# Four phases of a two-layer decoder step re-ordered: where selection rounds, normalised tiles, compression products and turned keys stand

## The reference

```
def layer_norm(x, g, b):                       # after each sub-layer
    mu = mean(x); var = mean((x - mu)**2)
    return (x - mu) * rsqrt(var + LN_EPS) * g + b

def compress(k, pe, w1, b1, w2):               # mixer C, once for keys, once for values
    ch = k in chunks of 16 tokens              # b c j g e
    ha = einsum('bcjge,jef->bcgf', ch, w1[:16])
    hb = einsum('bcjge,jef->bcgf', ch, w1[16:])
    const = einsum('je,jef->f', pe, w1) + b1
    h = gelu(ha[:, :-1] + hb[:, 1:] + const)
    return einsum('bcgf,fe->bcge', h, w2)

kc = compress(k rows, pe[0], ...); vc = compress(v rows, pe[1], ...)
pc = masked_softmax(q . kc * SCALE)            # 16 heads, 8 to a kv head
o_cmp = pc . vc                                # compressed branch
blocks = top_k(block sums of pc + bonus, 16)   # picks for the selected branch
o = g0 * o_cmp + g1 * o_selected + g2 * o_window
```

## Time and profile before

| | us |
|---|---|
| median of three runs | 2809.2 (2801.62 to 2817.05) |
| profiled execution | 2816.06 |
| its span | 2814.3 |
| sample_b | 371.6 to 613.3 |
| ffn0 | 986 to 1479.7 |
| compressed branch and its turning | 1615.1 to 1715.8 |
| sample_c | 1879.4 to 2226.2 |
| ffn1 | 2320 to 2807.4 |

### The profile page before, as it was taken

One profiled execution on the slowest core, in us unless ns is written; L12 is line 12 of the kernel. 1 busy time (PEld: TensorE's weight loads), 2 busy tenths in 40 slices (PEclk: granted clock), 3 DMA queues, 4 the chain that ended last, 5 costly groups with the idle time before them and its releaser, 6 DMA issues. The chain is left out here.

```text
span 2814.3 us, 41116 instructions
## 1 busy us (share of the span) xinstructions
PE 2243.7 (80%) x15442; PEld 1833.4 (65%) x15442; DVE 1336.9 (48%) x2667; ACT 910.1 (32%) x1497; POOL 140.7 (5%) x405
## 2 busy tenths in 40 slices
PE   5895755547767789998977777967888778999896
PEld 1895323325535689997867775545666568999784
DVE  2222437874656435554452215853444544555444
ACT  0210222211236235453331104752333313454332
POOL 0001000000000111110010000000000011111001
PEclk9997767768889889999988857987999888999998
DMA  2455166513132065564204232124333206656321
GB/s 62 139 189 176 25 207 225 188 49 144 66 120 93 9 195 200 194 212 139 79 8 134 91 50 68 54 82 116 128 136 136 75 6 196 209 191 222 119 76 41
DMA packets 166928, 341.04 MB, mean 121 GB/s; under 512 B 37726, under 2 KB 104334, under 8 KB 162810
## 3 DMA queue, kind: packets, MB, share of 16 engines
q1 hardware_dynamic: 151584, 200.99, 23.0%
q10 hardware_dynamic: 11756, 83.75, 8.6%
q0 software_dynamic: 3456, 54.53, 5.0%
HBM read 312.33 MB, written 97.35 MB: 146 GB/s over the span
## 5 line engine op out<-in xcount | busy, mean ns | idle before, releaser
L216 PE MATMUL ffn_acc<-x_h,ffn_wh 128*128 128x288 f32 x1408 | 303.8, 297 | 6.0 <-DVE ffn_wl L208 6.0
L216 PE MATMUL ffn_acc<-x_l,ffn_wh 128*128 128x288 f32 x1408 | 302.9, 297 | 0.0
L216 PE MATMUL ffn_acc<-x_h,ffn_wl 128*128 128x288 f32 x1408 | 302.9, 297 | 0.0
L216 PEld LDWEIGHTS ffn_acc<-x_h,ffn_wh 128*128 128x128 f32 x1408 | 228.8, 190 | 6.2 <-issue 6.2
L216 PEld LDWEIGHTS ffn_acc<-x_l,ffn_wh 128*128 128x128 f32 x1408 | 228.7, 190 | 0.0
L216 PEld LDWEIGHTS ffn_acc<-x_h,ffn_wl 128*128 128x128 f32 x1408 | 228.5, 190 | 0.0
L1720 PE MATMUL ffn_acc<-ffn_wh,x_h 128*128 128x512 f32 x440 | 175.4, 399 | 22.1 <-DVE ffn_wl L208 22.1
L208 DVE TENSOR_TENSOR ffn_wl<-ffn_w,ffn_wh 128x2048 fp32r<-128x2048 f32 (+1 forms) x88 | 154.3, 1755 | 69.8 <-ACT ffn_wh L1748 69.8
L1721 PE MATMUL ffn_acc<-ffn_wl,x_h 128*128 128x512 f32 x440 | 173.2, 394 | 0.0
L1722 PE MATMUL ffn_acc<-ffn_wh,x_l 128*128 128x512 f32 x440 | 173.1, 393 | 0.0
L208 DVE TENSOR_TENSOR x_l<-ffn_hid,x_h 128x1152 fp32r<-128x1152 f32 x44 | 59.8, 1358 | 165.1 <-ACT x_h L1806 165.1
(11 more groups left out here) (409 smaller groups left out, 4744.7 us busy)
## 6 DMA issues: line engine op xcount, KB each, us to landing
out_s_b_kv<-state_b_kv ACTq DMA_DIRECT2D x80, 768.0 KB, 7.8
ffn_w<-ffn_up SPq DMA_DIRECT2D x44, 1024.0 KB, 10.5
ffn_w<-ffn_down SPq DMA_DIRECT2D x44, 512.0 KB, 3.7
sb_k<-state_b_kv SPq DMA_DIRECT2D x8, 2048.0 KB, 11.5
sb_v<-state_b_kv SPq DMA_DIRECT2D x8, 2048.0 KB
proj_ab_w<-w_in_ab SPq DMA_DIRECT2D x11, 1024.0 KB, 5.3
proj_c_w<-w_in_c SPq DMA_DIRECT2D x7, 1024.0 KB, 5.5
hT_ab<-proj_ab_stage ACTq DMA_DIRECT2D x22, 288.0 KB, 2.1
```

The lines of the kernel that those rows point to most:

```text
L216: done = pe.matmul(o, weights, x, start=start, stop=stop)
```

## The change

Four parts, in four phases.

1. *sample_b_phase*: `select` takes a first round and a number of rounds. Per request two rounds stand behind the shift, one behind the copies of `pT`, one behind the scaling; `mix_in` of a request follows at once instead of behind the next shift.
2. *ffn_phase*: the down-products of the last three groups (`LATE`) run with the tile as the outer loop. VectorE takes tile `t` in, then the factors of `t - 1`, then the gain of `t - 2`; ScalarE the root of `t` and the scaling of `t - 1`. The turns of ffn0 follow after all.
3. *prompt_compressed_phase*: `w1` and `pe` are loaded at the end of the projection's SyncE queue (`load_phi`). Key branch and value branch stand in the two halves of the partitions; 64 products of 65 columns, the 65th being `pe`, give hidden sums and constant at once. Scores take two heads a product (8 of 128 rows a tile), two tiles ahead; the values come out turned and ScalarE copies them to `mixT`, so `mix_c` and `turn_mix_phase` go.
4. *sample_c_phase*: a third bank `tps`; the hidden sums go into two of the three logit banks; the `x` turns are spread among the score products of the request before; the second half of the hidden products alternates with the key turns ahead of the probabilities; GpSimd copies the value part of `kv` (128x2048) to `v`, and the next gather into that buffer waits for this copy and the key turns, not for the values. ScalarE copies keys ahead of the gelu.

```diff
@@ sample_b_phase, VectorE
-                if b:
-                    mix_in(b - 1)
-                    select(dve, b, 0)
+                select(dve, b, 0, 2)
                 dve.wait_ge(turned_p, b + 1)
...
-                select(dve, b, 1)
+                select(dve, b, 2, 1)
...
                 dve.tensor_scalar(o[:, :], outp, rinv[:, b % 2:b % 2 + 1], None, ALU.mult).then_inc(scaled, 1)
-            mix_in(NB - 1)
+                select(dve, b, 3, 1)
+                mix_in(b)
@@ ffn_phase, TensorE
+            for n in range(NF - LATE):
                 pe.wait_ge(d_low, 2 * n + 2)
                 for j in range(2):
                     for t in range(NT):
+                        last = down(n, j, t)
...
             pe.wait_ge(tail_out, NF // 2)
+            for t in range(NT):
+                for n in range(NF - LATE, NF):
+                    if t == 0:
+                        pe.wait_ge(d_low, 2 * n + 2)
+                    for j in range(2):
+                        down(n, j, t)
@@ ffn_phase, VectorE
-            for t in range(NT):
-                take_in(1, t)
-                dve.wait_ge(summed, NT + t + 1)
-                norm.statistics(dve, t, 1)
-                norm.aggregate(dve, t, NT + t + 1)
-            for t in range(NT):
-                norm.factors(dve, t)
-            for t in range(NT):
-                norm.gain(dve, t)
+            for t in range(NT + 2):
+                if t < NT:
+                    take_in(1, t)
+                    dve.wait_ge(summed, NT + t + 1)
+                    norm.statistics(dve, t, 1)
+                    norm.aggregate(dve, t, NT + t + 1)
+                if 1 <= t <= NT:
+                    norm.factors(dve, t - 1)
+                if t >= 2:
+                    norm.gain(dve, t - 2)
@@ prompt_compressed_phase
+def load_phi(nc, sp, io, w1, x, loaded):
+        for a in range(2):
+            r = slice(a * HD, (a + 1) * HD)
+            sp.dma_start(w1[r, :, :], io["phi_w1"][a].rearrange("j e f -> e j f")).then_inc(loaded, 16)
+            sp.dma_start(x[r, 2 * SEQ:], io["phi_pe"][a].rearrange("j e -> e j")).then_inc(loaded, 16)
...
-                for j in range(32):
-                    last = pe.matmul(psc[0:HD, a:a + 1], w1e[:, a, j, :], peT[:, a, j:j + 1], start=(j == 0), stop=(j == 31))
...
+            for j in range(2 * STRIDE):
+                for a in range(2):
+                    r = slice(a * HD, (a + 1) * HD)
+                    last = pe.matmul(psh[r, 0:2 * CH + 1], w1[r, j, :], x[r, j:j + STRIDE * 2 * CH + 1:STRIDE], start=(j == 0), stop=(j == 2 * STRIDE - 1))
...
-                for h in range(N_HEADS):
-                    last = pe.matmul(lgp[i % 2][:, h * 32:(h + 1) * 32], q[:, h, i * P:(i + 1) * P], kcT[:, h // 8, :], start=True, stop=True)
+                for m in range(KC):
+                    last = pe.matmul(lgp[i % 2][:, m * 64:(m + 1) * 64], q[:, m, i * P:(i + 1) * P],
+                                     kc[:, m // 4, :, :].rearrange("r two c -> r (two c)"), start=True, stop=True)
...
+                    for half in range(2):
+                        r = slice(half * HD, (half + 1) * HD)
+                        last = pe.matmul(out[half][:, u * P:(u + 1) * P], v_blk[r, u // 2, :], pT[r, i % 2, u * P:(u + 1) * P], start=True, stop=True)
@@ sample_c_phase
-            e.wait_ge(tps_out[n % 2], n // 2 + 1)
+            e.wait_ge(tps_out[n % 3], n // 3 + 1)
...
+            for c in range(NB):
+                pool.wait_ge(kv_in[c % 2], 16 * (c // 2 + 1))
+                if c:
+                    pool.wait_ge(slc_out, c)
+                pool.tensor_copy(v[:, :, :], kv[:, c % 2, :].rearrange("p (j n) -> p j n", j=STRIDE)[:, :, 384:512]).then_inc(v_ready, 1)
+                if c + 2 < NB:
+                    pool.wait_ge(v_ready, c + 1)
+                    n = turn_no[("k", c, 3)]
+                    for m in range(n - 2, n + 1):
+                        pool.wait_ge(tps_turned[m % 3], m // 3 + 1)
+                    gather(c + 2)
...
+                    for f in range(4):
+                        hidden(c, 1, f)
+                        turn_k(c, f)
                 if b >= 0:
                     turn_p(b, 0)
```

More of the change, by code:

```diff
@@ L1119, in sample_b_phase, with select @@
         selection = SampleSelection(p, score)
[L1121 to L1125, removed]
+        def select(dve, b, first, rounds):
+            each = selection.ROUNDS // NB
+            for r in range(first, first + rounds):
+                selection.round(dve, b * each + r)
         block = p.body.enter_context(nc.Block())
@@ L1407, in low_part @@
                      self.keep.xh[:, 4 * half:4 * half + 4, lo:lo + w]).then_inc(self.low, 1)
[L1410 to L1430, removed]
 def output_phase(nc, name, w_out, g, b, keep):
@@ L1708, in turn_tail, with down @@
                 last.then_inc(tail_turned, 1)
-            for n in range(NF):
+            def down(n, j, t):
                 h, f2 = divmod(n, NF // 2)
+                f = 2 * f2 + j
+                if h and f == 0:
+                    pe.wait_ge(summed, t + 1)
+                tile = slice(t * P, (t + 1) * P)
+                wide, part = (wdh[:, n % 4, j, :], wdl[:, n % 4, j, :]), (hh[:, n % 3, j, tile], hl[:, n % 3, j, tile])
+                pe.matmul(down_acc[t][:, :], part[0], wide[0], start=(f == 0), stop=False)
+                pe.matmul(down_acc[t][:, :], part[0], wide[1], start=False, stop=False)
+                last = pe.matmul(down_acc[t][:, :], part[1], wide[0], start=False, stop=(f == NF - 1))
+                if f == NF - 1:
+                    last.then_inc(product, 1)
+                return last
+            for n in range(NF - LATE):
                 pe.wait_ge(d_low, 2 * n + 2)
                 for j in range(2):
-                    f = 2 * f2 + j
                     for t in range(NT):
[L1716 to L1725, removed]
+                        last = down(n, j, t)
+                if n % (NF // 2) < NF // 2 - 1:
                     last.then_inc(wd_used, 1)
@@ L1951, in prompt_compressed_phase @@
         tps = p.ps("tps", [P, 512])
-        outp = p.ps("outp", [P, 2 * 512])
-        names = ("loaded", "gated", "const_sum", "const", "hidden", "activated", "keyed", "values", "cleared", "placed",
-                 "scored", "soft", "exped", "weighed", "turned", "copied", "attended", "mixed")
-        (loaded, gated, const_sum, const, hidden, activated, keyed, values, cleared, placed,
-         scored, soft, exped, weighed, turned, copied, attended, mixed) = (p.sem(n) for n in names)
+        out = [p.ps(f"out{i}", [P, 512]) for i in range(2)]
@@ L2159, in sample_c_phase @@
             if b + 1 < NB:
-                turns += [("x", b + 1, i) for i in range(8)]
+                turns += [("x", b + 1, i) for i in range(8)] + [("k", b + 1, i) for i in range(4)]
             if b >= 0:
@@ L2395, in _ @@
                 if c < NB:
-                    for f in range(4):
-                        hidden(c, 1, f)
-                    for i in range(4):
-                        turn_k(c, i)
                     turn_kw(c)
@@ L2454, in _ @@
                 if c < NB:
+                    for i in range(4):
+                        turned(("k", c, i), kT[:, i * 512:(i + 1) * 512])
+                    act.copy(kT[:, PAST:LS], k_new[:, 0, c * NS:(c + 1) * NS]).then_inc(kT_new, 1)
                     for a in range(2):
```

318 lines of the change are left out of this document (167 added, 151 removed).

## The result

The changed kernel takes 2693.27 us (median of 4, 2687.19 to 2699.18) against 2812.03 of the kernel before (median of 4); the ratio is 0.958, 95% interval 0.955 to 0.962: 119 us less, where 107.5 were forecast (2704, range 2675 to 2750). Measured again beside other kernels (last experiment) the ratio was 0.957 (0.955 to 0.959). The profiled execution took 2687.2 us, its span 2685.4.

| phase | before | after | difference | forecast |
|---|---|---|---|---|
| sample_b | 241.7 | 208.5 | -33.2 | -29 |
| ffn0, first to last work | 493.6 | 488.0 | -5.6 | -4 |
| compressed branch, first load to the next phase's | 101.3 | 58.3 | -43.0 | -46 |
| sample_c | 346.8 | 314.8 | -32.0 | -21 |
| ffn1, first to last work | 487.2 | 478.6 | -8.6 | -7.5 |

What follows compares the result with a forecast made beforehand. Barrier-closed phases on one core, each priced by itself: VectorE bounds sample_b, TensorE sample_c, serial tails the rest. -29 - 11.5 - 46 - 21 = -107.5 gives 2708.6 from 2816.1, 2701.7 from 2809.2; forecast 2704, range 2675 to 2750.

Steps and rivals of the forecast that it cites:

- sample_b, -29: In sample_b, moving one selection round per request into VectorE's wait cuts the period from 26.60 to 22.5 us; -29 us.
- the hole: In sample_b, VectorE's 4.73 us idle time per request ahead of the shift, while TensorE does the logit products.
- Rival (e): In sample_b, rounds move but key loads or ScalarE's copies keep the period at 26; nothing gained, 2733; chance 0.05.
- Feed-forward tails, -11.5: Serial work behind each feed-forward phase's last product shortens: ffn1 -7.5 us, ffn0 about -4, together -11.5.
- TensorE's wait: In each feed-forward phase, TensorE waits about 1.05 us for the last hidden group's high and low parts before tile 0.
- Compressed branch, -46: Prompt's compressed branch loses one-column products, a wait and the turning phase; next phase loads at 1669.3, not 1716.4; -46 us.
- Rival (b): In the compressed branch, quarter products don't run beside one another: 7 us more in hidden products, 0.8 a tile; 2714; chance 0.12.
- sample_c, -21: In sample_c, a third bank and earlier key copies remove waits for ScalarE's copies: -3 us a period, seven periods, -21.
- the slow stretch: In sample_c, 6.9 us of each period at granted clock 0.51; a period of 36.2 us if it stays, 33.2 at full clock.
- Rival (a): In sample_c, the slow stretch stays, from thinly spaced products around the picks: -1.4 a period, 11 us less gain, 2715; chance 0.17.
- (c): In sample_c, GpSimd's value copy of 8.7 us holds up VectorE's pair sum ahead of the picks: 26 lost, 2730; chance 0.08.
- (d): In sample_c, GpSimd's copy at 25 ns a column makes a 57 us loop against 37.6: +140 us, 2865; chance 0.03.

Runs made afterwards that it cites:

- last experiment: The changed kernel itself, run again on the same chip beside two kernels with respread sample_b rounds: 2693.82 us, ratio to before 0.957.
- the experiment on their order: Changed kernel with all 32 key-quarter products ahead of all 32 value-quarter products, not alternating: products 14.24 us against 7.44, branch 65.7 instead of 58.3.
- the two orders put back: Changed kernel with sample_c's third score products again ahead of the importance and x turns again in pairs: 2713.7 us, phase 339.3 instead of 314.8.
- one order alone: Kernel before, only sample_c's third score products moved behind the window's values of the request before: 2817.9 us, phase 349.1.

## Why the forecast held, and where its terms were off

*sample_b, -29, measured -33.* The step held: one round fills the hole, and the wait ahead of the shift is gone. Mis-sized was the period, 22.5 for 21.84: the logit products were taken at the 4.5 us of the earlier trace rows, and the copies of the turned probabilities at 17 behind the scaling; the granted clock in the phase is 0.87 after and was 0.76, so the shift begins 5.28 us behind the scaling and not 5.75, and the copies stand at 16.4 and, in four of the seven periods, wait for nothing. Rival (e) falls, since the period moved with the rounds.

*Feed-forward tails, -11.5, measured -14.* TensorE's wait was 1.06 us, as forecast. The gains were taken at 2.01 us each; two of the three took 1.23 and 1.21, since GpSimd's part was over by then or within 0.1 us of it, and the tails are 1.6 and 1.1 us shorter than forecast.

*Compressed branch, -46, measured -43* (58.3 us from its first load to the next phase's, 54 forecast). The steps held up to the last tile: hidden products 7.44 for 7.0, first softmax 21.4 us behind the first load for 20.6, 8.9 us a tile for 9.1. Missed was a queue: the last tile's exponential stands on ScalarE behind the copy of the third tile's turned probabilities, and VectorE waits 2.36 us for it; turn, values and barrier took 6.97 us for 5.3, 1.7 more than taken. Rival (b), quarters that take turns, falls with the experiment on their order.

*sample_c, -21, measured -32 to -36.* This is the term that was mis-sized, by its step "if the slow stretch stays, it is 36.2; between -4.4 and -1.4 I take -3": a midpoint between two outcomes, of which one came about. The stretch did not stay at all; the period is 32.8, as laid out for full clock (33.2; a turn with its hidden products took the 1.68 us taken). Rival (a), that the stretch stays, did not come about, and its reading of the stretch does not hold: the products in it weren't thin, TensorE is busy 6.43 of the 6.90 us of the earlier trace rows. The idle time ahead of them is the better candidate, for with the two orders put back the gaps and the stretch come again together; but one period with 4.5 us of idle time ran at full clock (1968.25 to 2003.68 above), so it is argued and not shown. And one step was wrong that the total could not show: of the two things said to take away the waits, the third bank does nothing. Which part of the new order takes away the wait for the keys was not run by itself.

*GpSimd's copy.* 1.89 us, near the memset of the earlier trace rows, not the 4 taken nor the bounds above. So (c) and (d) did not come about; (c)'s mechanism is real and has a margin of 3 us, the time between the copy's end and the pair sum.

## What to carry to other kernels

In a phase that TensorE bounds, price the waits and the granted clock apart: compare a period with the slow stretch and one without it in the same kernel (37.98 and 35.43 us here). Look at the idle gaps ahead of a slow stretch before blaming the products in it, and check in the profile that a moved product really filled a gap: the one moved by itself here filled none, and its run could not decide what it was made for. When a bound goes, lay out the chain that is late next before moving more work off the old one: a round less on VectorE was worth 1.1 us a period until the turn was moved too. A copy on an idle engine is free only as long as it ends before the other engine's short instructions that it lengthens (0.63 us to 3.51 here).

## What the runs showed of the hardware that was not expected

- Three VectorE instructions on 16 partitions, 0.63 us together, took 3.51 while GpSimd's copies of 1.9 us ran, one of them a TENSOR_SCALAR with a single input from SBUF (0.17 to 0.92).
- GpSimd copies 128x2048 numbers, read in strides, in 1.89 us, 0.9 ns a column; its small copies in the feed-forward phase take 0.403 for 16 columns, of which 16 columns would be some 0.015 by the larger copy's rate (an estimate).
- 64x64 products of two diagonal quarters took half the time when they alternated (7.44 for 14.24 us; at a granted clock of 0.50 in both, 50 products against 25 in 2.5 us).
- With the same instructions, one period of sample_c took 35.43 us at a granted clock of 1.00 and the next 37.98 at 0.91 in the mean (one order alone, in the kernel before).
